# Differential heads beside the last projections, and value tiles first in the linear-attention mixer

## The reference

```
for l in range(2):
    if l % 2 == 0: mix = diff_moba_mixer(x, ...)     # 4 differential heads, 4 block heads
    else:          mix = gla_mixer(x, ...)           # gated linear attention, 4 heads
    x = layer_norm(ALPHA * x + mix, ...)
    x = layer_norm(ALPHA * x + sqrelu_mlp(x, w1, w2), ...)
# a differential head: two softmax maps p0, p1; w = p0 - lam * p1; o = rms_norm(w @ v)
# a block head: one softmax map (256 tokens are one block, so plain causal attention)
# gla: o = rms_norm(decayed causal product of q, k, v) * silu(r); mix = o @ w_out
```

## Time and profile before

| what | us |
|---|---|
| median of 3 runs (lowest, highest) | 1717.49 (1708.98, 1719.38) |
| profiled execution, its span | 1713.44, 1711.6 |
| PE busy, its share | 1380.6, 81% |
| DVE busy, its share | 1131.3, 66% |
| ACT busy, its share | 539.2, 32% |

### The profile page before, as it was taken

The page is one execution under the profiler, slowest core; times in us unless marked ns, Lnnn a source line. Parts: engine busy times, 40 slices in busy tenths (PEclk is TensorE's granted clock), DMA queues, the critical chain, the costliest instruction groups (busy, mean ns, idle before and its releaser), DMA issues.

```text
span 1711.6 us, 17345 instructions
## 1 busy us (share of the span) xinstructions
PE 1380.6 (81%) x6264; PEld 971.9 (57%) x6264; DVE 1131.3 (66%) x2051; ACT 539.2 (32%) x1023; POOL 454.7 (27%) x393
## 2 busy tenths in 40 slices
PE   6976788777777677777777788658999899789998
PEld 5875668523223232222222267547999687679996
DVE  6655665688887788886555556647756659577564
ACT  2453434222221213212111233323434246234341
POOL 1154305244443443544444200000211025001110
PEclk9988899999998999999999989878999999889999
DMA  9554526799999999999999823204555534245550
GB/s 367 190 184 148 196 74 227 293 421 409 421 421 412 421 408 382 400 422 420 422 421 421 344 75 123 98 25 142 182 196 197 189 110 147 75 151 179 188 197 25
DMA packets 116629, 433.17 MB, mean 253 GB/s; under 512 B 6832, under 2 KB 7088, under 8 KB 83520
## 3 DMA queue, kind: packets, MB, share of 16 engines
q0 software_dynamic: 36864, 268.45, 38.0%
q1 hardware_dynamic: 79392, 162.51, 26.8%
q10 hardware_dynamic: 288, 1.11, 0.2%
HBM read 431.00 MB, written 1.05 MB: 252 GB/s over the span
## 4 chain that ended last, share of the span: by engine, by line
PE 47%; DMA 23%; DVE 19%; ACT 6%; issue 2%; POOL 2%; SPq 0%; DVEq 0%; ACTq 0%; POOLq 0%
PE PS L45 45%; DMA EB<-in_experts,EI 22%; DVE EB L78 5%; DVE WL L75 3%; ACT BIG L24 2%; PE PS L84 1%; DVE X L63 1%; POOL W L75 1%; ACT WH L24 1%; DVE Y L75 1%; DMA W<-in_w_ada 1%; DVE GV L75 1%; DVE EB L63 1%; DVE XL L75 1%; DVE ST L69 1%
## 5 line engine op out<-in xcount | busy, mean ns | idle before, releaser
L45 PE MATMUL PS<-EB,BIG 128*128 128x512 f32 x1024 | 495.4, 628 | 169.9 <-ACT BIG L24 169.8
L45 PEld LDWEIGHTS PS<-EB,BIG 128*128 128x128 f32 x1024 | 190.3, 197 | 470.3 <-ACT BIG L24 287.3
L78 DVE CUSTOM_DVE_ANT_0 EB<-EB,Y 128x1024 f32<-128x1024 f32 x256 | 313.4, 1224 | 146.0 <-DMA EB<-in_experts,EI 145.0
L39 POOL DMA_INDIRECT EB<-in_experts,EI x256 | 288.3, 1126 | 397.0 <-PE PS L45 380.9
L75 DVE TENSOR_TENSOR WL<-W,WH 128x1024 fp32r<-128x1024 f32 x228 | 297.5, 1351 | 109.5 <-ACT WH L24 109.3
L45 PE MATMUL PS<-XH,WH 128*128 128x256 f32 x928 | 272.0, 293 | 12.8 <-DVE WL L75 10.0
L24 ACT ACTIVATE WH<-W 128x1024 fp32r<-128x1024 f32 x240 | 237.8, 1047 | 91.8 <-PE PS L45 84.9
L45 PE MATMUL PS<-XL,WH 128*128 128x256 f32 x928 | 265.0, 286 | 0.0
L45 PE MATMUL PS<-XH,WL 128*128 128x256 f32 x928 | 265.0, 286 | 0.0
L45 PEld LDWEIGHTS PS<-XH,WH 128*128 128x128 f32 x928 | 180.9, 195 | 17.9 <-DVE WL L75 11.1
L45 PEld LDWEIGHTS PS<-XL,WH 128*128 128x128 f32 x928 | 180.8, 195 | 2.7 <-issue 2.4
(11 more groups left out here) (170 smaller groups left out, 1512.1 us busy)
## 6 DMA issues: line engine op xcount, KB each, us to landing
W<-in_ffn_w SPq DMA_DIRECT2D x32, 2048.0 KB, 8.8
W<-in_w_ada SPq DMA_DIRECT2D x12, 2048.0 KB, 12.2
W<-in_w_in SPq DMA_DIRECT2D x6, 2048.0 KB, 12.9
W<-in_hy_w_in SPq DMA_DIRECT2D x6, 2048.0 KB, 13.5
W<-in_gla_w_in SPq DMA_DIRECT2D x6, 2048.0 KB, 7.9
W<-in_w_query SPq DMA_DIRECT2D x4, 2048.0 KB, 8.2
W<-in_w_out SPq DMA_DIRECT2D x2, 2048.0 KB, 8.3
EB<-in_experts,EI POOLq DMA_INDIRECT x256, 11.1
```

The costliest lines, as they stand in the source:

```text
L39: return lambda e: e.indirect_dma_start(*a, **k)
L45: return lambda e: e.matmul(*a, **k)
L78: return lambda e: e.tensor_tensor_reduce(*a, **k)
```

## The change

Rotations are put in a list and done behind the first group of the next pair (`rotate_one`). From the tenth of the sixteen projection groups on, each hook runs a step of the differential heads; the block heads follow alone, in other buffers, with the norm of the differential heads between their steps. The output projection does the differential half of its contraction first for all four groups, then the block half. `hyt[5]` and the tiles behind it change their high-part buffers. In GLA the value tiles come first, those of token tile 0 ahead of the turning of tile 1; the levels go by half groups of the two gate tiles that are left. At its end token tile 0 is turned and multiplied ahead of tile 1. `bank()` skips a bank that is being filled.

```diff
@@ -232,8 +232,13 @@
         bank_free = [() for _ in range(8)]
         turn = [0]
+        filling = set()
+
         def bank():
             b = turn[0] % 4
+            while b in filling:
+                turn[0] += 1
+                b = turn[0] % 4
             turn[0] += 1
             return b
...
@@ -299,9 +304,9 @@
         w_ada(11, 0)
         first_block_tiles = len(tiles)
         last_in_wh.clear()
-        for j, s, h in ((2, 2, 0), (5, 1, 1), (0, 0, 2), (1, 3, 0), (3, 2, 1), (4, 1, 2)):
+        for j, s, h in ((2, 2, 0), (5, 1, 1), (0, 0, 2), (1, 3, 0), (3, 2, 1), (4, 1, 0)):
             hyt.append(wplan(A["hy_w_in_2"], 0, j * 512, s, h))
-        later_w, later_h = itertools.cycle((0, 3, 2, 1)), itertools.cycle((0, 1, 2))
+        later_w, later_h = itertools.cycle((0, 3, 2, 1)), itertools.cycle((1, 0, 2))
         def wplan_on(ap, r0, j):
             return wplan(ap, r0, j * 512, next(later_w), next(later_h))
...
         ffn_tiles = [plan_ffn(0)]
-        gla_in = {j: wplan_on(A["gla_w_in_2"], 0, j) for j in (0, 1, 4, 5, 2, 3)}
+        gla_in = {j: wplan_on(A["gla_w_in_2"], 0, j) for j in (2, 3, 0, 1, 4, 5)}
         gla_out = [wplan_on(A["gla_w_out_2"], 0, j) for j in range(2)]
         ffn_tiles.append(plan_ffn(1))
...
             for c in range(0, 4, 2):
                 b = bank()
+                filling.add(b)
                 for j in range(2):
                     w = slice((c + j) * 128, (c + j + 1) * 128)
                     tk = dense(PS[b][:, j * 256:(j + 1) * 256], tile, fm_pairs(tile, w), *tokens, *bank_free[b], xtok=xtok)
                     if j == 1:
                         bank_free[b] = evac(b, c, tk)
+                        filling.discard(b)
                     tick(n)
                     if hook:
...
                 q, u = RB[i], RC[i]
                 ta = act(lambda e: e.activation(q, PS[b][:, :], ACT.Copy), tk, *rb_free[i])
-                b2 = bank()
-                t2 = mm(PS[b2][:, :], [(rot, q)], ta, t_k2, *bank_free[b2])
-                two = lambda a: a.rearrange("p (c t) -> p c t", c=2)
-                both = lambda a: a.unsqueeze(1).broadcast_to([128, 2, 256])
-                dve(lambda e: e.tensor_tensor(two(u), two(PS[b2][:, :]), both(sn), ALU.mult), t2, *rb_free[i])
-                bank_free[b2] = (dve.last,)
-                dve(lambda e: e.tensor_tensor(two(q), two(q), both(cs), ALU.mult))
-                final(two(q), two(u), c)
-                rb_free[i] = (dve.last, t2)
+
+                def rotate():
+                    b2 = bank()
+                    t2 = mm(PS[b2][:, :], [(rot, q)], ta, t_k2, *bank_free[b2])
+                    two = lambda a: a.rearrange("p (c t) -> p c t", c=2)
+                    both = lambda a: a.unsqueeze(1).broadcast_to([128, 2, 256])
+                    dve(lambda e: e.tensor_tensor(two(u), two(PS[b2][:, :]), both(sn), ALU.mult), t2, *rb_free[i])
+                    bank_free[b2] = (dve.last,)
+                    dve(lambda e: e.tensor_tensor(two(q), two(q), both(cs), ALU.mult))
+                    final(two(q), two(u), c)
+                    rb_free[i] = (dve.last, t2)
+                turning.append(rotate)
                 return (ta,)
             return f
+
+        turning = []
+
+        def rotate_one(latest=0):
+            while len(turning) > latest:
+                turning.pop(0)()
         def fin_split(q, u, c):
...
-        fm_tile(hyt[5], evac_rope(r128, c128, s128, fin_to(KM)))
-        t_proj = fence()
         diff_done, moba_done = {}, {}
-        part = lambda a, n: [a[:, i * 384:(i + 1) * 384] for i in range(n)]
-        diff = attention(4, lambda i: QD[:, i, :], lambda i: KD[:, i // 2, :],
-                         lambda h, t: V[:, t, h * 128:(h + 1) * 128], 128, 4, 0.125, [buf(i) for i in range(6)], [buf(i) for i in range(6, 9)],
-                         maps=2, lam=lam, tokens=t_proj, done=diff_done)
+        fresh = [0]
+
+        def behind_group():
+
+            fresh[0] += 1
+            if fresh[0] % 2:
+                rotate_one()
+            if fresh[0] == 10:
+                mixing.append(attention(4, lambda i: QD[:, i, :], lambda i: KD[:, i // 2, :],
+                                        lambda h, t: V[:, t, h * 128:(h + 1) * 128], 128, 4, 0.125,
+                                        [buf(i) for i in range(6)], [buf(i) for i in range(6, 9)],
+                                        maps=2, lam=lam, tokens=(act.last, dve.last, *hyt[2].done), done=diff_done))
+            if fresh[0] >= 10:
+                next(mixing[0], None)
+
+        mixing = []
+        fm_tile(hyt[2], evac_rope(r64, c64, s64, fin_split), *t_xt, hook=behind_group)
+        fm_tile(hyt[3], evac_rope(r64, c64, s64, fin_to(KD)), hook=behind_group)
+        fm_tile(hyt[4], evac_rope(r128, c128, s128, fin_to(QM)), hook=behind_group)
+        fm_tile(hyt[5], evac_rope(r128, c128, s128, fin_to(KM)), hook=behind_group)
+        rotate_one()
+        t_rope = (dve.last, act.last)
+        for _ in mixing[0]:
+            pass
         moba = attention(4, lambda i: QM[:, i, :], lambda i: KM[:, i, :],
                          lambda h, t: V[:, t, 512 + h * 128:512 + (h + 1) * 128], 128, 6, 128.0 ** -0.5,
-                         part(GVf[:, 2688:3840], 3), [*part(BIG[:, 5120:5888], 2), buf(9)], tokens=t_proj, base=16, done=moba_done)
-        mixers = [diff, moba]
-        while mixers:
-            for g in list(mixers):
-                if next(g, True):
-                    mixers.remove(g)
-            tick(2)
-
...
+                         [buf(i) for i in (9, 0, 1, 2)], [buf(i) for i in (3, 4, 5)], tokens=t_rope, base=16, done=moba_done,
+                         taken=lambda: (diff_done["out"],))
+
+        def write_diff(t):
+            if t:
+                return act(lambda e: e.activation(Y[:, t, 0:512], PS[4 + t][:, :], ACT.Copy), diff_done["out"], *t_rope)
+            return dve(lambda e: e.tensor_copy(Y[:, t, 0:512], PS[4 + t][:, :]), diff_done["out"], *t_rope)
+
+        def write_moba(t):
             td = dve(lambda e: e.tensor_tensor(
                 Y[:, t, 512:1024].rearrange("p (h d) -> p h d", h=4), PS[6 + t][:, :].rearrange("p (h d) -> p h d", h=4),
-                SMA[:, 16 + t:24:2].unsqueeze(2).broadcast_to([128, 4, 128]), ALU.mult), moba_done["out"])
+                SMA[:, 16 + t:24:2].unsqueeze(2).broadcast_to([128, 4, 128]), ALU.mult), moba_done["out"], *t_rope)
             bank_free[6 + t] = (td,)
-            t_moba = turn_half(Y[:, t, :], t, 1, td)
...
-        t_xt = (t_moba, t_diff)
+            t_moba[t] = turn_half(Y[:, t, :], t, 1, td, None, 6 + t)
+
+        t_moba = {}
+        diff_steps, diff_x = norm_half(0, write_diff, 4, 1e-5, subln)
+        steps = collections.deque(diff_steps)
+        for _ in moba:
+            for _ in range(2):
+                if steps:
+                    steps.popleft()()
+            tick(2)
+        while steps:
+            steps.popleft()()
         up_first = ffn_tiles[0][0][0, 0]
         wh_free[up_first.index] = (diff_done["out"], moba_done["out"])
         wh_held.clear()
...
-        def close_mixer(l, pair, t_xt):
-            norm = layer_norm(A["ln_mix_g_2"][l], A["ln_mix_b_2"][l])
-            close_pair(pair, norm, *t_xt)
-            return norm.tokens
-
-        t_xt = close_mixer(0, hy_out, t_xt)
+        norm = layer_norm(A["ln_mix_g_2"][0], A["ln_mix_b_2"][0])
+        groups = {}
+        for t in range(2):
+            for j in range(2):
+                b = bank()
+                groups[j, t] = b
+                take(hy_out[j])
+                dense(PS[b][:, :], hy_out[j], tm_pairs(hy_out[j], t), diff_x["x", t], *bank_free[b], ks=range(4), stop=False)
+                if (j, t) == (0, 0):
+                    write_moba(0)
+                    write_moba(1)
+                else:
+                    tick(2)
+        for t in range(2):
+            for j in range(2):
+                b = groups[j, t]
+                tk = dense(PS[b][:, :], hy_out[j], tm_pairs(hy_out[j], t), t_moba[t], ks=range(4, 8), start=False,
+                           mid=norm.mid if (j, t) == (1, 1) else None)
+                if t == 1:
+                    wdone(hy_out[j], tk)
+                norm.give(j, b, t, tk)
+        t_xt = norm.tokens
         f = (pe.last, dve.last, act.last)
         wg = GVf[:, 2176:2304]
...
-        ffn(0, t_xt, norm, beside=lambda free: wg_parts.append(narrow_parts(wg, 16, 0, t_wg, *free)))
+        ffn(0, t_xt, norm, beside=lambda free: wg_parts.append(narrow_parts(wg, 16, 0, t_wg, *free)), turn=False)
+        first_v = []
+        for j in range(2):
+            b = bank()
+            take(gla_in[2 + j])
+            first_v.append((b, dense(PS[b][:, :], gla_in[2 + j], tm_pairs(gla_in[2 + j], 0), norm.xt[0], *bank_free[b])))
+        norm.last()
         t_xt = norm.tokens
-        f = (dve.last, act.last)
         QG = BIG[:, 0:1024]
         KG = BIG[:, 1024:2048]
```

(61 more changed lines are left out.)

35 lines of the change are left out of this document (8 added, 27 removed).

## The result

The changed kernel takes 1744.76 us (median of 4 runs, 1742.24 to 1747.11) against 1715.83 before: ratio 1.0177, 95% interval 1.0145 to 1.0208. (All ratios are the estimates on record, each against runs of the kernel before in the same session; the quotient of two medians can differ from them by 0.001.) It is slower by over 1%, where 1721 and "within 1%" were forecast; the time lies 7 us above the range. The profiled execution took 1747.11 us, its span 1745.0 (before 1711.6), so 33.4 us are to be placed.

The account below looks back on a forecast made before the run. TensorE was taken to bound the projections, TensorE and VectorE the level part, with waits and chains elsewhere. -4+10.8-0.6 = +6 us gave 1719.6 profiled, 1723.5 on the median; forecast 1721, within 1%, eight in ten within 1697 and 1738.

Parts of the forecast that it names:

- Part 1: Differential/block mixer: rotations later, differential heads beside the last projections; -4 us, bounds -12 and +4.
- The projections with rotations: From 1031.15 us on: 14 projection groups, 39.3 us, 8 rotations, 9.0, and the last wait; sum 51 us.
- 17.9 us of stalls: Differential heads beside projections: TensorE waits of 1.7 ahead of first scores, then 5.5, 4.3, 5.5 and 0.9 us.
- rival (a): Faster: hooks hide the heads' work, stalls ahead of transposes under 1.5 us, part 1 -22, 1690 us; chance 0.18, full or half.
- The second term: Differential heads beside projections: TensorE's drop to 1.2 GHz after long stalls, charged at 3 us.
- the dearer account: Low clock charged 2 us after each of three long stalls, nothing hidden: 6 us, part 1 ending at -1.
- Part 2: Linear-attention mixer: value tiles first, level steps twice as dense in the gate tiles; +10.8 us, bounds -8 and +22.
- 13.3 to 15 us a round: Level part: a chain of two level steps through TensorE, ScalarE and VectorE; four rounds within 61 us from keys to heads.
- rival (b): Slower: level rounds take 18 us, not 14, through GpSimd interference and TensorE at 1.2 GHz; 1737 us; chance 0.17.
- The 20 us more: Level part: cost over seven levels if each operand were held for a full GpSimd decay instruction; not charged.
- Part 3: End of the linear-attention mixer by token tile: -0.6 us, bounds -5 and +2.
- Stalls that the granted clock doubles: Sign that would show the forecast wrong, as would a level part under 50 us.

Follow-up runs that it names:

- x4: Kernel before the change, with only the rotations put off, each behind the next half group of projections: 1704.28 us, ratio 0.9939.
- x9: Kernel before with part 1 alone, each differential head's weights issued right behind its own maps, a step earlier: 1701.46 us, ratio 0.9925.
- x7: Kernel before with part 2 alone, level step issued ahead of each gate group's evacuation and split pieces: 1715.83 us, ratio 1.0016.
- x3: Kernel before with part 3 alone, the end of the linear-attention mixer by token tile: 1712.36 us, ratio 0.9992.

## Why the prediction was wrong

The failed steps are two terms of the sum: part 1's stalls with their clock, and part 2's round.

**Part 1: -4 forecast, +11.0 in the trace, +8 alone.** The projections with rotations were too dear, not too cheap: 51 us forecast, 47.0 in x4. The forecast counted 14 groups from 1031.15 on, where 13 are left once the first wait is hidden (2.8 us), so the 3.2 us of that wait were not credited; and a rotation in a row of matmuls costs PE 0.86 us from start to start (1065.60 to 1066.46), where I charged the 1.13 from its start to its very end.

The step that failed is "17.9 us of stalls". Measured: 4.1, 5.9, 4.3, 5.8 and 6.1, 26.2 us. I had 1.7 for the first, where PE waits for ScalarE's and VectorE's pieces of a split issued just before, and 0.9 for the fifth, where I had no split pieces ahead of the weights. The three in the middle were right to 0.4 us. The mechanism had been named, with rival (a)'s condition against it; the walk of the queue was not carried through the pieces that `tick` puts there.

The second term is the clock, of which I charged 3 us. The block heads came at 1125.2 and not at 1110.4. Of these 14.8 us 8.3 are stalls; the projections being over-priced by 4, that leaves 10.6 for the low clock and for the heads' own work, and the row of x9 puts 7.5 on the clock (41.6 less 34.0). There the dearer account set beside the Trainium skill's rule (TensorE: Matmul & The Clock Gate, Part 1), an estimate of 2 us after each of three long stalls, was nearer than mine, and still too cheap. The block heads took 26.5 us as walked, the output projection with its norm 41.1 and not 38; what took these 3 us is not shown. Rival (a) came near by one order: x9 has waits of 0.4, 2.7, 1.4 and 3.3 us (two of them under its 1.5), and part 1 is a gain of 13 us, not the 22 that (a) had; 10 of the 13 are there with the rotations alone.

**Part 2: +10.8 forecast, +23.2 measured.** The keys end 54.2 us after the feed-forward's last matmul, forecast 54.3; the 6.6 us gap is gone, but for 1.4. The failed step is "13.3 to 15 us a round": 16.3, 19.0 and 18.0, so that the level part took 75.7 us and not 61. (The terms listed for a round add up to 12.7 to 14.6, without ScalarE's split piece of 0.96, which stands in the chain too, and the 61 us have room for four rounds of 13.3 and hardly more. 54.3 and 61 make 115.3, not 115.5.) That is rival (b), with its mechanism: two split pieces 4.18 where I took 2.35 to 3.3, products and half group 6.3 to 7.6 us on PE where I took 4.8, since the clock is 0.78 and not 0.99 (products of 1.95 us take 3.44 and 3.79 behind a wait), and VectorE standing still 20.5 us in four waits, once 2.65 and three times around 6, where (b) said that over 5 decides it. I gave it 0.17. The argument against it, the clock of 0.99 there before, was worth nothing: before, PE was busy 61.3 of 67.6 us, and the very chain I described takes that away. The prediction also took the Trainium skill's exclusion (SBUF — State Buffer, Who interferes with whom) by one row, a pair of operands, and did not work it out for the split pieces, which have two SBUF inputs too. Here they take 4.17 a pair beside GpSimd's decays and 2.35 without, so the rule pointed the right way, but by 0.9 us a piece and not by a whole decay instruction of 1.95. The 20 us more that I had worked out from it are not what happened: x7 has pairs of 4.18 and 2.44 us too and is 20 us faster.

**Part 3: -0.6 forecast**, -1.5 in the trace, -1.6 in that of x3, by the times of x3 not told from nothing.

Of the signs named, the three waits ahead of the transposes (there were four), the gap at the feed-forward's end and the 52 us behind the heads came as said, the last a half us shorter. The others did not: block heads at 1108 to 1114 (1125), the feed-forward at 1174 to 1181 (1193), waits of 2 to 4 us for ScalarE (one of four), 60 to 66 us of levels (76). "Stalls that the granted clock doubles" was named as what would make it wrong; the clock did make them dearer, though not twice as dear.

## What to carry over

When work is put into hooks between an engine's groups, walk every queue entry by entry, with what the split and evacuation helpers put in; what the other engine waits for goes directly behind what makes it ready, not to the step that uses it. Here VectorE waiting 1.1 us for its own input saved 21 us.

Where steps are packed twice as densely, look for a cycle through three queues before adding up busy times: in the level part no engine was busy for more than two thirds of the time, and the round was still 18 us. An evacuation that starts with a wait belongs behind the work that is ready.

A part that is slower as a whole can hold a gain: run each alone before all are dropped. Here it was the rotations, 10 us by themselves.

## What the runs showed of the hardware

- TensorE did not fall to the lower level by the length of one wait alone. In x9 the matmuls behind a wait of 2.70 us stood 0.21 us apart, those behind a later one of 3.33 us 0.12:

```profile
1075.01 0.41 PE L45 MATMUL PS<-XH,WH 128*128 128x256 f32 x1
1075.22 0.41 PE L45 MATMUL PS<-XL,WH 128*128 128x256 f32 x1
...
1091.49 0.28 PE L45 MATMUL PS<-XH,WL 128*128 128x256 f32 x1
1091.61 0.28 PE L45 MATMUL PS<-XH,WH 128*128 128x256 f32 x1
```

- The VectorE part of a split piece (two inputs in SBUF, 128x1024) took 1.18 us with GpSimd idle and 2.09 beside its decays; a pair of operands 1.42 and up to 2.86.
- A rotation (a plain fp32 product of 512 columns, two records in the trace) cost 0.86 us from start to start in an unbroken row of matmuls; from its start to the end of its last record it took 1.02 there, and 1.13 behind a wait.
